# Two kinds of DMA stores issued from ScalarE's queue instead of SyncE's, in a two-layer transformer kernel with dense product-key experts

## What is computed

```python
q = (xt @ w_q).reshape(PEER_TBLOCK, PEER_HEADS, 2, PEER_HALF)
s = jnp.einsum('thpd,hpnd->thpn', q, sub_keys).astype(jnp.float32)
s1, i1 = lax.top_k(s[:, :, 0], PEER_TOPK)
s2, i2 = lax.top_k(s[:, :, 1], PEER_TOPK)
...
top, pos = lax.top_k(cand, PEER_TOPK)
eidx = jnp.take_along_axis(cidx, pos, axis=-1)
gates = jax.nn.softmax(top, axis=-1)
act = jax.nn.gelu(jnp.einsum('td,thkd->thk', xt, u[eidx]).astype(jnp.float32), approximate=False)
return jnp.einsum('thk,thkd->td', (gates * act).astype(xt.dtype), v[eidx])
```

## Time and profile before

| What | Value |
|---|---|
| Time, median of 3 runs | 3115.41 us |
| Time of the profiled execution | 3111.95 us |
| Its span (first to last instruction) | 3110.0 us |
| PE busy | 3021.6 us, 97% |
| DVE busy | 2407.8 us, 77% |
| POOL busy | 1310.9 us, 42% |
| ACT busy | 1193.4 us, 38% |
| DMA traffic | 800.86 MB, mean 258 GB/s |
| Activation stores | 256 of 192 KB, median 7.4 us from issue to landing |
| Gate stores | 24 of 2 MB, median 15.9 us from issue to landing |

### The profile page before, as it was taken

How to read it: one execution, slowest core, us unless ns; L and a number is a source line. 1 busy time by engine, 2 the same in 40 slices (tenths; PEclk the granted TensorE clock), 3 DMA queues, 4 the chain that set the end, 5 groups by cost and what they waited for, 6 DMA issues and landing times.

```text
span 3110.0 us, 44566 instructions
## 1 busy us (share of the span) xinstructions
PE 3021.6 (97%) x16468; PEld 2672.1 (86%) x16468; DVE 2407.8 (77%) x4496; ACT 1193.4 (38%) x1842; POOL 1310.9 (42%) x749
## 2 busy tenths in 40 slices
PE   7999999999999999999998979999999999999998
PEld 5657899999998888887787967899999998888887
DVE  5345899988877888888235876899888978888887
ACT  4433333444433333333333433333444433333333
POOL 3313465444434444443344423465444444444442
PEclk9999999999999999999998989999999999999999
DMA  3202367999999999998221002367999999999996
GB/s 136 73 21 96 99 201 253 341 375 356 374 365 376 372 355 351 356 348 293 88 95 48 1 28 95 102 201 265 336 379 357 373 368 389 361 349 362 351 357 254
DMA packets 345719, 800.86 MB, mean 258 GB/s; under 512 B 27936, under 2 KB 191776, under 8 KB 345248
## 3 DMA queue, kind: packets, MB, share of 16 engines
q1 hardware_dynamic: 271776, 529.55, 48.9%
q0 software_dynamic: 73728, 268.47, 22.7%
HBM read 695.15 MB, written 102.76 MB: 257 GB/s over the span
## 4 chain that ended last, share of the span: by engine, by line
PE 92%; DVE 3%; DMA 2%; ACT 1%; issue 1%; POOL 0%; SPq 0%; ACTq 0%; DVEq 0%
PE PS L1361 27%; PE PS L1363 27%; PE PS L1362 27%; PE PS L1529 3%; PE PS L1626 2%; PE PS L1601 2%; DMA arena<-acts_dram 1%; DVE arena L1327 1%; PE PS L1506 1%; PE PS L1484 1%; DMA acts_dram<-arena 1%; PE PS L1467 1%; PE PS L1466 0%; POOL w_lo L509 0%; DMA w_raw<-in_mla_t 0%
## 5 line engine op out<-in xcount | busy, mean ns | idle before, releaser
L1361 PE MATMUL PS<-x_hi,w_hi 128*128 128x384 f32 (+1 forms) x2616 | 924.9, 354 | 14.7 <-issue 7.5
L586 ACT ACTIVATE w_hi<-w_raw 128x1024 fp32r<-128x1024 f32 x609 | 643.0, 1057 | 699.5 <-PE PS L1363 685.4
L1363 PE MATMUL PS<-x_hi,w_lo 128*128 128x384 f32 (+1 forms) x2616 | 908.3, 347 | 0.0
L1362 PE MATMUL PS<-x_lo,w_hi 128*128 128x384 f32 (+1 forms) x2616 | 907.0, 347 | 0.0
L520 POOL DMA_INDIRECT arena<-in_v_t,arena x256 | 445.1, 1738 | 599.5 <-DVE resid L1173 551.0
L1361 PE MATMUL PS<-w_hi,x_hi 128*128 128x512 f32 x1744 | 682.1, 391 | 12.8 <-POOL w_lo L509 8.6
L1362 PE MATMUL PS<-w_lo,x_hi 128*128 128x512 f32 x1744 | 680.2, 390 | 0.0
L1363 PE MATMUL PS<-w_hi,x_lo 128*128 128x512 f32 x1744 | 679.9, 390 | 0.0
L509 POOL TENSOR_TENSOR w_lo<-w_raw,w_hi 128x1024 fp32r<-128x1024 f32 x169 | 417.7, 2476 | 616.1 <-ACT w_hi L586 616.1
L1150 DVE TENSOR_TENSOR w_lo<-w_raw,w_hi 128x1024 fp32r<-128x1024 f32 x440 | 537.2, 1221 | 107.2 <-ACT w_hi L586 106.9
L520 POOL DMA_INDIRECT arena<-in_u_rows,arena x256 | 380.5, 1486 | 487.7 <-DVE arena L1157 434.5
(11 more groups left out here) (178 smaller groups left out, 2483.7 us busy)
## 6 DMA issues: line engine op xcount, KB each, us to landing
w_raw<-in_u_t SPq DMA_DIRECT2D x256, 512.0 KB, 6.9
w_raw<-in_v_t SPq DMA_DIRECT2D x256, 512.0 KB, 6.7
acts_dram<-arena SPq DMA_DIRECT2D x256, 192.0 KB, 7.4
gates_dram<-arena SPq DMA_DIRECT2D x24, 2048.0 KB, 15.9
arena<-gates_dram SPq DMA_DIRECT2D x64, 768.0 KB, 7.4
arena<-acts_dram SPq DMA_DIRECT2D x256, 192.0 KB, 7.1
w_raw<-in_hg_t SPq DMA_DIRECT2D x40, 512.0 KB, 3.2
w_raw<-in_pq_t SPq DMA_DIRECT2D x32, 512.0 KB, 3.2
```

The lines of the kernel that those rows point to most:

```text
L586: act.activation(w_hi[:, slot, :], w_raw[:, slot, :], ACT.Copy).then_inc(hi_ready, 1)
L1361: pe.matmul(ps, wh, xh, start=start, stop=False)
L1362: pe.matmul(ps, wh, xl, start=False, stop=False)
L1363: return pe.matmul(ps, wl, xh, start=False, stop=stop)
```

## The change

The activation stores and the gate stores leave SP's list and enter ACT's. On ACT, step s of the u pass is now: moves of quads, Gelu s, `high` of tile s + 4, store of activation s, and a gate store when the quads moved up to this step complete one. The conditions they wait for are the same ones, and the buffers, sizes and patterns too. SP's list has only loads, with the wait for all gate stores still at step 127.

```diff
--- before.py
+++ after.py
@@ -443,18 +443,6 @@
                     .then_inc(sem("far_gain_in"), 16)
                 load_range(f"pq{layer}", 16 - RING, RING)
 
-                def store_act(c):
-
-                    sp.wait_ge(gelu_done, NKEYS * layer + 4 + c + 1)
-                    sp.dma_start(acts_dram[c], act_st[:, c % RING, :]).then_inc(act_stored[c % RING], 16)
-
-                def store_gates(h):
-
-                    sp.wait_ge(gate_moved, 4 + QUADS * layer + HALF_QUADS * (h + 1))
-                    sp.dma_start(
-                        gates_dram[:, :, h].rearrange("g p f t -> p g (f t)"),
-                        gate_st[:, h % 2].rearrange("p g f t -> p g (f t)")).then_inc(gate_stored[h % 2], 16)
-
                 def load_act(c):
 
                     sp.wait_ge(act_stored[c % RING], 16 * (NKEYS // RING * layer + c // RING + 1))
@@ -469,17 +457,11 @@
                     sp.dma_start(gate_ld[:, g % 2].rearrange("p h f t -> p (h f t)"),
                                  gates_dram[g].rearrange("p h f t -> p (h f t)")).then_inc(gate_loaded[g % 2], 16)
 
-                stored = 0
                 for s in range(2 * NKEYS + 8):
                     if s < NKEYS:
                         load_tile(bu + s, u[s], (bu + s) % RING)
                     elif s < 2 * NKEYS:
                         load_tile(bv + s - NKEYS, v[s - NKEYS], (bv + s - NKEYS) % RING)
-                    if 8 <= s < NKEYS + 8:
-                        store_act(s - 8)
-                    if stored < HALVES and quads_before(s - 8) >= HALF_QUADS * (stored + 1):
-                        store_gates(stored)
-                        stored += 1
                     if s == NKEYS - 1:
                         for b in range(2):
                             sp.wait_ge(gate_stored[b], 16 * (HALVES // 2) * (layer + 1))
@@ -735,6 +717,17 @@
                         PS[:, 4 + q % 4, :].rearrange("p (t e) -> p e t", t=4),
                         ACT.Copy, scale=1.0 / GATE_UNIT).then_inc(gate_moved, 1)
 
+                def store_act(c):
+
+                    act.wait_ge(gelu_done, NKEYS * layer + 4 + c + 1)
+                    act.dma_start(acts_dram[c], act_st[:, c % RING, :]).then_inc(act_stored[c % RING], 16)
+
+                def store_gates(h):
+
+                    act.wait_ge(gate_moved, 4 + QUADS * layer + HALF_QUADS * (h + 1))
+                    act.dma_start(gates_dram[:, :, h].rearrange("g p f t -> p g (f t)"),
+                                  gate_st[:, h % 2].rearrange("p g f t -> p g (f t)")).then_inc(gate_stored[h % 2], 16)
+
                 def far_gelu_of(b):
 
                     part = slice(b * HK // 4, (b + 1) * HK // 4)
@@ -752,6 +745,7 @@
                                    product[:, c % RING, :].rearrange("p (t n) -> p t n", n=P),
                                    ACT.Copy).then_inc(sem("product_high"), 1)
 
+                stored = 0
                 for s in range(2 * NKEYS):
                     if s == ROUTES_AT - 4:
                         act.wait_ge(sem("top_less_max"), TT * (layer + 1))
@@ -761,6 +755,11 @@
                             move_gates(q)
                         gelu(s)
                     next_high(bu + s)
+                    if s < NKEYS:
+                        store_act(s)
+                    if stored < HALVES and quads_before(s + 1) >= HALF_QUADS * (stored + 1):
+                        store_gates(stored)
+                        stored += 1
                     for b in range(4):
                         if s == dots_done_by((b + 1) * HK // 4) + 1:
                             far_gelu_of(b)
```

## The result

The changed kernel takes 3182.02 us (median of 4 runs, 3178.63 to 3185.98) where the kernel before takes 3114.95 us: ratio 1.0214, 95% interval 1.0196 to 1.0232, so 67 us slower. I had forecast 3118 us and a range up to 3148, with 0.37 on slower. The sign came out against the likeliest case and the time lies outside the range. The mechanism that cost the time is the one priced in part 3 of the prediction; its size is nearer rival A's, and more than that.

The account below looks back on a forecast made before the run. PE, busy 97% of the span, was taken to bound the kernel. 3111.95 - 4.3 (passage from u to v) + 6.8 (holds on ACT) = 3114.5, plus 3.5 from profiled execution to median: 3118 us; range 3110 to 3148.

Parts of the forecast that it names:

- part 3: ACT's list, u pass: holds behind gate stores make octets late; 6.8 us of PE waits, bounds 2.4 to 16.5.
- rival A: Longer holds on ACT as SP's loads share the DMA engines: 3132 us with one load, 3157 with two; chance 0.28.
- The bound on the gain: Only PE's waits for the product's low part hang on the stores: at most 4.3 us of 3112.
- the six waits of 4.3 us: PE's waits for the product's low part, passages from u to v, both layers together; expected to go.
- part 4: Passage from u to v: v tiles start 6 to 11 us earlier; -4.3 us, bounds 0 and -4.3.
- part 1: ACT's queue: 256 activation and 24 gate store issues, 122 us, cost 0 under ACT's idle time; at most 110 us uncovered.
- my two bounds on the cover: Hold length above which PE waits for an octet: 11.4 or 13.5 us by place; 12.5, the middle, taken.
- Rival B: Shorter holds, by 2 us, as the gate store no longer queues behind SP's load: 3112 us; chance 0.16.
- Rival C: SP held by ACT's gate store, its loads 1 to 2 us late at 22 places: 3145 us at worst; chance 0.06.

Follow-up runs that it names:

- the four-part version: Changed kernel with each gate store sent as four DMAs of 512 KB, one per step; 3110.28 us, ratio 0.9980 to the kernel before.
- the pause: Changed kernel with SP waiting until a gate store has landed before it sends the next tile; 3124.87 us, ratio 1.0018 to the kernel before.
- one tile beside: Changed kernel with SP sending one tile after each gate store's issue, then waiting until it has landed; 3150.27 us, ratio 1.0109 to the kernel before.

## Why the prediction was wrong

The bound on the gain held in the profiles: the six waits of 4.3 us are all that the u passes of any version got back. By the medians the four-part version gained 6 us (0.9980, 0.9971 to 0.9989), somewhat more than the bound; see below. The passage from u to v (part 4) gained little in the changed kernel, where 4.5 us of waits for `x_lo` and `w_lo` stay there (behind the last hold, by their place; not tried alone); in the version that defers activation stores all six waits are gone, and its ratio is 0.9983. So the -4.3 us of the sum were 0.2 us the other way in the changed kernel.

Issue work (part 1): right, shown by the version with 256 issues on ACT at 0.9999.

The hold in ACT's list (part 3): right in place and mechanism, down to the 5.8 us from ACT's release to the octet. The step that failed is its size. I took the holds of before, 11.7 us, as the likeliest and got 6.8 us of waits. With holds of 11.8 us on ACT, which is what the pause makes, 3.7 us of waits and a ratio of 1.0018 were measured, so the sum for that hold was near (I had 1.001), in part by luck: the waits were half of what I had, and the gain at the passage was 0.9 us and not 4.3. But in the changed kernel the hold is 15.8 us, since SP, no longer held itself, sends two tiles and more beside the gate store. Rival A named this and priced it at 14.6 us of hold and 46 us of waits; 43.6 us of waits were measured. That the two agree is luck, since two misses cancel. The hold was 1.2 us longer than rival A had it, and the cover was larger than the 12.5 us that I took: the 22 holds of the changed kernel exceed 12.5 us by 69 us together and 13.5 us by 47 us; with one tile beside it is 38 and 20 us, and 20.1 us of waits were measured. So the upper of my two bounds on the cover, 13.5, was nearer. I gave rival A 0.28, because I thought SP would soon be without a slot and because the load ahead of the store was gone. SP did run out of slots, but after two tiles, and those are what made the holds longer.

What no case had is the clock, a term that I left out without a reason: most waits of PE of over 2 us are followed by 3 to 6 us at the 1.2 GHz level, in all 20 us, on top of the 43.6. With it rival A's 3157 would have been 3177, 5 us from the measured 3182. The range's upper end, 3148, took in rival A with one tile (3132) and left out rival A with two tiles (3157), the case that came.

Rival B (shorter holds) is out: 15.8 us. Rival C (loads late) had SP held by ACT's gate store; SP isn't held.

Open: the four-part stores gain 0.2% over the kernel before, of which the profiles show about 2 us in the u passes; the rest is within what the profiles of single executions scatter. What decides, beside a wait's length, whether the clock falls behind it stays open (3.24 and 3.23 us, 0.71 and 1.00). And no run changed the row size of the gate store: whether its 4096 rows or its 2 MB make the hold wasn't tried.

## What to carry to other kernels

A big DMA in short rows (here 2 MB in rows of 512 bytes) can hold the next DMA of the same queue, here until 12 to 16 us after its issue; look at the length of the DMA issued after it, not at its own, and give it a queue with no compute behind it, or cut it to pieces that drain before the next issue, or send nothing behind it for that long. Moving it to another queue frees the first queue, and the first queue's transfers then make the hold longer: price the hold with them beside it. Of an in-order engine, the cover of a delay is the slack of the tightest thing queued behind it (here an octet's 3.8 us), and waits of PE cost more than themselves through its clock: 43.6 us of them cost 20 us on top here.

## What the runs showed of the hardware

- A hold belongs to the issuing queue: SP's loads took 0.33 us each while ACT's queue stood for 12.15 us behind a 2 MB store in 512-byte rows.
- Its length follows what else uses the DMA engines: 11.8, 14.3 and 15.8 us with 0.2, 1.3 and 2.3 tiles of 512 KB on average sent beside it.
- It passes with time: a DMA asked for 13.7 us after the gate store took 0.33 us at one place; at others up to 6.3 us were left.
- Ten of twelve waits of PE of 2.4 to 4.1 us were followed by 3 to 6 us at the 1.2 GHz level (granted clock 0.71 to 0.86 over the next 10 us), none of four of 0.95 to 1.5 us; this was 20 of 64 us.
- Half the size wasn't half the hold: two 1 MB stores in successive steps held the queue until 14.2 to 20.6 us after the first.
